# Up projection with the two activation halves as one 512-column operand, and the last modulation sums over eight blocks

## What is computed

```python
mod = c_act @ w_mod[l] + b_mod[l]                    # 2048 x 12288 weights, one row vector
sh1, sc1, gt1, sh2, sc2, gt2 = split(mod, 6)
...
h = x * (1.0 + sc2) + sh2                            # 256 x 2048
gate, up = _split(h @ w_up[l], (D_FF, D_FF))         # D_FF = 5632
f = silu(_causal_dwconv(gate, conv_w[l], conv_b[l])) * up     # width 3, causal
x = _layer_norm(DEEPNORM_ALPHA * x + (1.0 + gt2) * (f @ w_down[l]), ln2_g[l], ln2_b[l])
```

## Time and profile before

| | us |
|---|---|
| runs | 1487.14, 1486.45, 1469.22 (median 1486.45) |
| profiled execution | 1470.31, span 1468.5 |
| PE busy over the span | 1345.5 (92%), mean granted clock 0.955 of full |
| DVE, ACT, POOL busy | 1008.6 (69%), 567.1 (39%), 157.3 (11%) |
| DMA | 319.05 MB, mean 217 GB/s |
| up projection, first to last matmul | 694.3 to about 1208 |

### The profile page before, as it was taken

One profiled execution on the slowest core, in us unless ns is written; L12 is line 12 of the kernel. 1 busy time (PEld: TensorE's weight loads), 2 busy tenths in 40 slices (PEclk: granted clock), 3 DMA queues, 4 the chain that ended last, 5 costly groups with the idle time before them and its releaser, 6 DMA issues.

```text
span 1468.5 us, 23741 instructions
## 1 busy us (share of the span) xinstructions
PE 1345.5 (92%) x9167; PEld 1238.6 (84%) x9167; DVE 1008.6 (69%) x1302; ACT 567.1 (39%) x791; POOL 157.3 (11%) x221
## 2 busy tenths in 40 slices
PE   1777689999999999899999999999999999999994
PEld 1676589999888768688999999999999998888883
DVE  4888797877788987557777777665555555545545
ACT  1222361333423444333544444434444444333331
POOL 3233111101011110100711010000000000000001
PEclk9788798999999999998999999999999999999997
DMA  8999985665566673863578787565556556766561
GB/s 318 330 332 332 322 279 172 217 201 174 180 199 212 216 259 124 300 213 117 160 242 283 249 306 248 172 184 162 185 157 206 180 184 193 251 192 194 175 211 57
DMA packets 142821, 319.05 MB, mean 217 GB/s; under 512 B 12110, under 2 KB 19616, under 8 KB 141728
## 3 DMA queue, kind: packets, MB, share of 16 engines
q1 hardware_dynamic: 114528, 213.23, 44.9%
q0 software_dynamic: 28224, 104.87, 20.9%
HBM read 315.97 MB, written 2.10 MB: 217 GB/s over the span
## 4 chain that ended last, share of the span: by engine, by line
PE 72%; DVE 15%; DMA 8%; issue 3%; ACT 2%; POOL 0%; SPq 0%; DVEq 0%; ACTq 0%; POOLq 0%
PE G L1378 63%; PE M L1378 9%; DMA MODR<-in_w_mod_dram 5%; DVE ACC L811 5%; DVE WLO L792 2%; DMA RAW<-in_w_out_dram 1%; DMA RAW<-in_w_in_dram 1%; PE M L1528 1%; ACT WHI L501 0%; DVE HLO L841 0%; DVE RN L904 0%; DVE X L1362 0%; DVE X L1371 0%; DVE HTMP L851 0%; DVE SM L1105 0%
## 5 line engine op out<-in xcount | busy, mean ns | idle before, releaser
L1378 PE MATMUL G<-HHI,WHI 128*128 128x256 f32 x1856 | 539.4, 291 | 11.7 <-DVE HLO L841 6.1
L1378 PE MATMUL G<-HLO,WHI 128*128 128x256 f32 x1856 | 530.7, 286 | 0.0
L1378 PE MATMUL G<-HHI,WLO 128*128 128x256 f32 x1856 | 530.4, 286 | 0.0
L1378 PEld LDWEIGHTS G<-HHI,WHI 128*128 128x128 f32 x1856 | 362.1, 195 | 16.2 <-issue 9.3
L792 DVE TENSOR_TENSOR WLO<-RAW,WHI 128x1024 fp32r<-128x1024 f32 x210 | 255.1, 1222 | 166.9 <-ACT WHI L501 163.9
L1378 PEld LDWEIGHTS G<-HLO,WHI 128*128 128x128 f32 x1856 | 362.2, 195 | 0.5 <-issue 0.5
L1378 PEld LDWEIGHTS G<-HHI,WLO 128*128 128x128 f32 x1856 | 361.7, 195 | 0.0
L501 ACT ACTIVATE WHI<-RAW 128x1024 fp32r<-128x1024 f32 x210 | 221.4, 1059 | 271.7 <-PE G L1378 205.0
L797 DVE TENSOR_TENSOR WLO<-RAW,WHI 128x1024 fp32r<-128x1024 f32 x174 | 217.8, 1272 | 141.1 <-ACT WHI L507 141.0
L507 ACT ACTIVATE WHI<-RAW 128x1024 fp32r<-128x1024 f32 x174 | 180.1, 1054 | 188.7 <-PE G L1378 145.1
L811 DVE SCALAR_TENSOR_TENSOR ACC<-MODR,SM,ACC 128x1024 f32<-128x1024 f32 x150 | 191.9, 1279 | 28.9 <-DMA MODR<-in_w_mod_dram 25.6
(11 more groups left out here) (269 smaller groups left out, 1389.5 us busy)
## 6 DMA issues: line engine op xcount, KB each, us to landing
MODR<-in_w_mod_dram POOLq DMA_DIRECT2D x192, 512.0 KB, 6.0
RAW<-in_w_up_dram SPq DMA_DIRECT2D x176, 512.0 KB, 4.5
RAW<-in_w_in_dram SPq DMA_DIRECT2D x88, 512.0 KB, 5.4
RAW<-in_w_down_dram SPq DMA_DIRECT2D x88, 512.0 KB, 4.0
RAW<-in_w_out_dram SPq DMA_DIRECT2D x32, 512.0 KB, 5.1
X<-in_x_dram SPq DMA_DIRECT2D x2, 1024.0 KB, 9.3
XR<-in_x_dram POOLq DMA_DIRECT2D x2, 1024.0 KB, 6.7
out_dram<-X SPq DMA_DIRECT2D x4, 512.0 KB, 2.7
```

The source lines that it names most:

```text
L1378: return pe.matmul(out_, l, r, start=start, stop=stop, skip_group_check=True)
```

## The change

Three things. First, `HHI` and `HLO` now lie side by side in one tensor `HH` of two 256-column halves for each k-tile, and the up projection issues two matmuls for a tile in place of three: high weight by both halves (512 columns, a whole bank), and low weight by the high half (256 columns, into the left half of the same bank). The right half of the bank holds the product of the low activations, which has to be added behind: a copy on ACT, an addition on DVE. The four tiles take four banks; the first half of a block uses G0 to G3, the second M0 to M3. Second, the last modulation sums go over blocks 1 to 8, one behind every fourth chunk, through two buffers; the sum over partitions is now inside block 9 and the spreading inside the first down block. Third, the loops: blocks 9 and 10 are written out, and so is the down projection on PE.

```diff
-UP_MODS = 4
+UP_MODS = 8
...
-    HHI = sb("HHI", [P, KT, T], 48, f32r)
-    HLO = sb("HLO", [P, KT, T], 64, f32r)
+    HH = sb("HH", [P, KT, 2, T], 48, f32r)
+    HHI, HLO = HH[:, :, 0, :], HH[:, :, 1, :]
...
-    ACC2, MODR2 = sb("ACC2", [P, 2, MOD_W], 160), sb("MODR2", [P, RING, MOD_W], 144)
+    ACC2, MODR2 = sb("ACC2", [P, 2, MOD_W], 168), sb("MODR2", [P, 2, MOD_W], 160)
...
 # POOL
-            pool.memset(ACC2[:, :, :], 0.0).then_inc(zeroed, 1)
...
             pool.wait_ge(h_lo, 2 * KT)
+            pool.memset(ACC2[:, :, :], 0.0).then_inc(zeroed, 1)
...
 # ACT, up_block
                         act.wait_ge(w_used, i * (2 * CH_IN) + (N0_UP + CH_IN))
+                        if early == 0:
+                            act.wait_ge(f_new, i)
+                        for k in range(4):
+                            act.activation(SF[:, k, :], G[k][:, T:2 * T], ACT.Copy).then_inc(b_cp, 1)
                         act.wait_ge(conv_cp, i + 1)
                         for k in range(4):
-                            act.activation(GF[:, k, :], G[k // 2][:, (k % 2) * T:(k % 2) * T + T], ACT.Identity,
+                            act.wait_ge(evac[0], i * 4 + (EV1[0] + k + 1))
+                            act.activation(GF[:, k, :], SF[:, k, :], ACT.Identity,
                                            scale=CONV[:, 4 + k:5 + k], bias=CONV[:, k:k + 1]).then_inc(g_pre, 1)
...
                     if j == 2 * CH_IN - 1:
+                        act.wait_ge(w_used, i * (2 * CH_IN) + (N0_UP + 2 * CH_IN))
+                        act.wait_ge(g_new, i + 1)
+                        for k in range(4):
+                            act.activation(SF[:, k, :], M[k][:, T:2 * T], ACT.Copy).then_inc(b_cp, 1)
                         act.wait_ge(x1_done, 16)
-                        act.wait_ge(evac[1], i * 2 + (EV1[1] + 2))
+                        act.wait_ge(f_new, i + 1)
                         act.activation(FHI[:, ds(i * 4, 4), :], GF[:, :, :], ACT.Copy).then_inc(f_hi, 1)
...
 # DVE, up_block
                     if j == CH_IN - 1:
+                        for k in range(4):
+                            dve.wait_ge(b_cp, i * 8 + (k + 1))
+                            dve.tensor_tensor(SF[:, k, :], G[k][:, 0:T], SF[:, k, :], ALU.add)\
+                               .then_inc(evac[0], 1)
...
-                        for k in range(2):
-                            dve.tensor_tensor(gf[:, 512 * k:512 * k + 512], G[2 + k][:, :],
-                                              gf[:, 512 * k:512 * k + 512], ALU.mult).then_inc(evac[1], 1)
...
+                        dve.tensor_tensor(GF[:, :, :], GF[:, :, :], SF[:, :, :], ALU.mult).then_inc(g_new, 1)
+                        for k in range(4):
+                            dve.wait_ge(b_cp, i * 8 + (k + 5))
+                            dve.tensor_tensor(SF[:, k, :], M[k][:, 0:T], SF[:, k, :], ALU.add)\
+                               .then_inc(evac[1], 1)
...
+                        dve.tensor_tensor(GF[:, :, :], GF[:, :, :], SF[:, :, :], ALU.mult).then_inc(f_new, 1)
...
+            up_block(UP_MODS + 1, False, cols=True)
             own[0], own[1] = n_own + OWN_UP * (UP_MODS + 2), None
-            two_parts(GT2)
             dve.wait_ge(mod_col, MOD_PARTS)
             gate_rows(GT2, DGM2)
...
 # PE
+            def fm_pairs(s, kk, kt, banks, start, stop):
+
+                for i in range(4):
+                    wh, wl = (w[:, s, kk, i * P:(i + 1) * P] for w in (WHI, WLO))
+                    mm(banks[i][:, :], wh, HH[:, kt, :, :], start=start)
+                    ins = mm(banks[i][:, 0:T], wl, HHI[:, kt, :], stop=stop)
+                return ins
...
-                            ins = fm(j % RING, kk, kt, out_pair(half), kt == 0, kt == KT - 1)
+                            ins = fm_pairs(j % RING, kk, kt, (G, M)[half], kt == 0, kt == KT - 1)
                         ins.then_inc(w_used, 1)
+                        if sums and half == 0 and j == CH_IN // 2:
+                            pe.wait_ge(mod_done, MOD_PARTS * KT)
+                            pe.wait_ge(evac[1], i * 4 + EV1[1])
+                            for m in (MOD_PARTS - 2, MOD_PARTS - 1):
+                                mod_reduce(m, ACC2, 8 * (m % 2))
...
+                    if b == 0 and j == 2:
+                        pe.wait_ge(evac[1], EV2[1])
+                        gate_rows(DGM2, 4, M)
```

More of the change, by code:

```diff
@@ L456, in last_parts @@
                 for k in ks:
-                    pool.wait_ge(mod_done, i * 8 + (MODS_IN + k - RING + 1))
-                    row, m = i * 4 + k // 2, MOD_PARTS - 2 + k % 2
-                    pool.dma_start(MODR2[:, k % RING:k % RING + 1, :], wm[:, ds(row, 1), m * MOD_W:(m + 1) * MOD_W])\
-                        .then_inc(mod_in[k % RING], 16)
-            last_parts(0, range(RING))
+                    pool.wait_ge(mod_done, i * 4 + (MODS_IN + k - 1))
+                    row, m = i * 2 + k // 2, MOD_PARTS - 2 + k % 2
+                    pool.dma_start(MODR2[:, k % 2:k % 2 + 1, :], wm[:, ds(row, 1), m * MOD_W:(m + 1) * MOD_W])\
+                        .then_inc(mod_in[k % 2], 16)
+            last_parts(0, range(2))
             pool.wait_ge(zn_pe, 8)
@@ L475, in _ @@
                         .then_inc(x1_done, 1)
-            last_parts(0, range(RING, 8))
+            last_parts(0, range(2, 4))
             with pool.Fori(1, UP_MODS) as i:
-                last_parts(i, range(8))
+                last_parts(i, range(4))
             for n in range(2):
@@ L1318, in up_block @@
                 assert own[0] - n_own == OWN_UP, own[0] - n_own
+            up_block(0, False, len(EARLY))
             dve.wait_ge(zeroed, 3)
[L1321 removed]
             with dve.Fori(1, UP_MODS + 1) as i:
                 up_block(i, True)
[L1324 to L1325 removed]
+            up_block(UP_MODS + 1, False, cols=True)
             own[0], own[1] = n_own + OWN_UP * (UP_MODS + 2), None
[L1327 removed]
             dve.wait_ge(mod_col, MOD_PARTS)
             gate_rows(GT2, DGM2)
[L1330 to L1331 removed]
+            up_block(UP_MODS + 2, False)
             own[0], own[1] = n_own + OWN_UP * N_UP, None
@@ L1755, in _, with up_block @@
                 ins.then_inc(zn_pe, 1)
-            def up_block(i, first=False):
+            def fm_pairs(s, kk, kt, banks, start, stop):
[4 more added lines that the diff above has]
+                return ins
+            def up_block(i, first=False, sums=False):
                 for half in range(2):
-                    pe.wait_ge(evac[half], i * (4, 2)[half] + EV1[half])
+                    pe.wait_ge(evac[half], i * 4 + EV1[half])
                     for j in range(CH_IN):
@@ L1769, in _ @@
+                    if sums and half == 0:
+                        pe.wait_ge(mod_col, MOD_PARTS)
             up_block(0, True)
-            with pe.Fori(1, UP_MODS + 2) as i:
+            with pe.Fori(1, UP_MODS + 1) as i:
                 up_block(i)
-            pe.wait_ge(mod_done, MOD_PARTS * KT)
-            for m in (MOD_PARTS - 2, MOD_PARTS - 1):
-                mod_reduce(m, ACC2, 8 * (m % 2))
+            up_block(UP_MODS + 1, sums=True)
             up_block(UP_MODS + 2)
-            pe.wait_ge(mod_col, MOD_PARTS)
@@ L1777, in _ @@
-            gate_rows(DGM2, 4, M)
-            with pe.Fori(UP_MODS + 3, N_UP) as i:
-                up_block(i)
             pe.wait_ge(f_lo, N_UP - 1)
-            with pe.Fori(0, N_DOWN_BLOCKS // 2) as i:
-                for bb in range(2):
-                    pe.wait_ge(evac[bb], i * 2 + EV2[bb])
-                    for j in range(CH_DOWN):
-                        n = bb * CH_DOWN + j
-                        pe.wait_ge(lo_done, i * (2 * CH_DOWN) + (N0_DOWN + n + 1))
-                        if bb == 0 and 2 * j + 2 > FT - 4:
-                            pe.wait_ge(f_lo, N_UP)
-                        for kk in range(2):
-                            kt = 2 * j + kk
-                            ins = tm(n % RING, kk, kt, out_pair(bb), kt == 0, kt == FT - 1, FHI, FLO)
-                        ins.then_inc(w_used, 1)
+            for b in range(N_DOWN_BLOCKS):
+                pe.wait_ge(evac[b % 2], b // 2 * 2 + EV2[b % 2])
+                for j in range(CH_DOWN):
+                    n = N0_DOWN + b * CH_DOWN + j
+                    pe.wait_ge(lo_done, n + 1)
+                    if b == 0 and 2 * j + 2 > FT - 4:
+                        pe.wait_ge(f_lo, N_UP)
+                    for kk in range(2):
+                        kt = 2 * j + kk
+                        ins = tm(n % RING, kk, kt, out_pair(b), kt == 0, kt == FT - 1, FHI, FLO)
+                    ins.then_inc(w_used, 1)
+                    if b == 0 and j == 2:
+                        pe.wait_ge(evac[1], EV2[1])
+                        gate_rows(DGM2, 4, M)
```

61 lines of the change are left out of this document (28 added, 33 removed).

## The result

Over 15 runs each, the changed kernel takes 1490.9 us in the median (1484.17 to 1501.04), the one before 1486.21 (1468.79 to 1490.92). The ratio is 1.0079, 95% interval [1.0047, 1.0111]: 7 to 16.5 us slower, where 5.6 us less was forecast. The means, 1491.8 and 1481.2 us, stand 10.6 us apart. The predicted 1464.7 us and the range up to 1488 both missed. The profiled execution of after took 1485.95 us, with a span of 1483.8.

The account below looks back on a forecast made before the run. The prediction took PE, busy without waits in the up projection, as the bound. It summed -18.8 (pairs) + 6.6 (first halves) + 4.8 (second halves) + 1.8 (block 9) = -5.6 us against 1470.3: 1464.7 us, range 1451 to 1488.

Parts of the forecast that it names:

- What PE saves: Up projection: 1408 triples of 360.0 ns become pairs of 346.7 ns, saving 18.8 us.
- The ordinary drains: Up projection half ends: PE waits 0.6 us at chunk 11, 0.6 at chunk 3 in eight blocks, 1.8 entering block 10.
- Eleven halves: 6.6: Drain behind each block's first half: PE waits 0.6 us at chunk 11, 6.6 us over eleven blocks.
- That `gate_rows` costs nothing: Behind the third down chunk: ACT's four copies fit while PE has two chunks, 5.4 us, in hand.
- The sums: Sums over partitions: 3.47 us, staying on PE's path, elsewhere but as long.
- What costs nothing: Step listing moved sums, `gate_rows`, modulation parts, weight loads, memset and written-out loops as adding no time.
- the loads: SP's queue of weight loads: the same in number and order, no cost.
- The memset: POOL's 1.8 us memset, now ahead of the residual's scaling: hidden, as the first `FHI` write comes later.
- The second: Rival: ACT's copies at half ends cost 564 ns, not 378; 0.75 us more at 20 places, 1479.7 us; chance 0.25.
- The third: Rival: in the up projection the pair saves nothing, the triple's time stays 360.0 ns; 1477.8 us; chance 0.08.
- The fourth: Rival: the 20 short waits pull PE's clock to 1.2 GHz, costing 55 us, about 1520; chance 0.04.
- The level: Whole kernel: point set from the profiled 1470.3 us; the median's 16 us above it kept for the range.

Follow-up runs that it names:

- e12: The kernel before, unchanged, traced once more; up projection 517.07 us against 514.01 in its first trace.
- e2: The changed kernel with three 256-column matmuls for a tile again; up projection 532.85 us, ratio to before 1.0113 [1.0058, 1.0169].
- e6: e5 plus a GpSimd pause until block 0's taps are done, its memset behind the scaling; ratio to before 0.9881 [0.9822, 0.9939].
- e13: e6 with two tiles' 512-column matmuls ahead of their 256-column ones, and the 16 sums spread over four chunks; ratio to before 0.9857 [0.9804, 0.9911].
- e5: The changed kernel with DVE's `gb_act` wait later, next-wanted splits ahead of drains, modulation parts moved two chunks; up projection 512.46 us.

## Why the prediction failed

By its steps:

- **What PE saves: half right.** The triple was 360.0, the pair 346.7 where the fixed part is 13.3 ns a matmul, as from the earlier trace rows. The second distance, 353.4, has no row in the trace of before, where all triples have one distance. It costs between nothing and 9.4 us; after's two traces show 6.6 and 3.1. The term of the sum, 18.8, was too large by that.
- **The ordinary drains: right.** Forecast 12.6 us for all but block 0, measured 14.1. A place costs 0.63 us at chunk 11 (0.6 forecast), 0.75 at chunk 3 (0.6) and 1.8 at the turn to block 10 (1.8).
- **"Eleven halves: 6.6" was wrong for one of eleven.** I took block 0 to be like block 9. It has GpSimd beside it, and the change moved the taps' input from PSUM to SBUF: 10.8 us in place of 0.6. I named the cheaper row as the open question ("if reading `SF` from SBUF is no quicker") and did not ask when it would be dearer. The row for it was in the trace of before: `split_lo` at 712.75 took 2.14 us and not 1.22.
- **That `gate_rows` costs nothing was wrong.** The cover that I named, two chunks of PE, was not in hand: DVE's wait for `gb_act` stood in program order ahead of the low part of the very next chunk. I added up ACT's work and never asked what was queued behind the wait on DVE. 3.4 us of wait and 1.9 of clock.
- **The sums, taken at their own 3.5 us:** after's trace has 3.3 us more, for the low clock. Before's second trace, e12, has 3.1 more than its first, so the forecast stood on the one execution that did not have it.
- **"What costs nothing", the loads:** they are the same in number, but two of them come later, and about 3 us of the lead were gained. The memset was hidden, as said.
- **Rivals.** The second had the direction, and its +9.4 us lies in the measured 7 to 16.5, but that is luck: it asked for 0.75 us more at each of 20 places, where a copy costs 0.39 us (378 ns in the earlier trace rows) and not 0.56, and the ordinary places came out as forecast. The third is refuted by e2. The fourth had the place wrong: no short wait lowered the clock (0.98 over the stage), but the waits of 8.0 and 3.4 us did.
- **The level.** The sum was made against 1470.3 us, the low end of before's runs. Two traces each give: up and rest 776.01 against 793.37 (+17.36), lead 99.82 against 97.00 (-2.82). That is +14.5 us, inside the measured 7 to 16.5. What comes ahead of the lead differs from run to run by up to 19 us in traces of all kernels (it ends between 590 and 609 us), which is what made after's profiled start look 5.8 us better. The range's upper end had no room for a loss on top of that spread.

What stays open: what at a restart decides between 346.7 and 353.4 ns, why the order in twos gives 696.7, and what decides whether the clock falls at the sums. That the change can pay is shown: with the edits of e6 the pair's saving comes through, 0.6 to 1.8% faster than before, and with e13's 0.9 to 2.0%.

## What to carry to other kernels

When an operand moves from PSUM to SBUF, look at what GpSimd does at that time, in each stage apart; the first block is not like the others. When work is moved past a wait, follow every engine's queue behind the new waiter: the chunk wanted next must be split ahead of it. Then put what PE wants next ahead of each drain; here that took 19 waits away.

## What the runs showed of the hardware

- Taps with both tensors in SBUF took 5.39 and 5.60 us for four beside GpSimd's tensor operations and 1.73 and 1.67 without; those with one in PSUM, 1.71 and 1.65 beside them. In the slow case the two engines took turns, one tap to one GpSimd operation.
- A 512-column and a 256-column matmul in turn started every 346.7 or 353.4 ns, constant between two waits and settled anew behind each, in two executions of one kernel differently. The difference of 6.7 ns is 16 cycles of 2.4 GHz; 6.2 of it lie between the 512-column start and the next one (e5: 236.2 and 117.1 ns; e6: 230.0 and 116.7). In twos: 696.7 ns for four. Equal 256-column ones, in five traces: 120.0 at the full clock.
- Behind the same 16 one-column sums the same kernel ran at a granted clock of 1.00 in one execution and 0.57 in another.
- The wait for weights in the output projection was 20.0 and 19.6 us in two traces, and between 14.1 and 17.1 in thirteen in which two 512 KB loads of another queue came later.
